# Attention of the first block: value matmuls with high and low halves side by side, and a shifted order of steps

## What is computed

```python
kc = rmsnorm(compress(heads(kcm, KVH), ...), ...)     # 31 compressed keys
vc = compress(heads(vcm, KVH), ...)                   # 31 compressed values
p_cmp = masked_softmax(einsum(q_nope, kc) * scale, cmp_mask)
o_cmp = einsum('bgntc,bgcd->bgntd', p_cmp, vc)
o_slc = selected_attn(q_rope, k_sl, heads(vsl, KVH), sel, scale)
o_win = window_attn(q_rope, k_wn, heads(vwn, KVH), scale)
o_nsa = gates[0] * o_cmp + gates[1] * o_slc + gates[2] * o_win
y_nsa = o_nsa * jax.nn.silu(nz)
```

## Time and profile before

| | us |
|---|---|
| median of 3 runs (lowest to highest) | 2809.46 (2808.98 to 2810.98) |
| profiled execution, its own time | 2808.89 |
| its span, first to last instruction | 2807.1 |
| PE busy | 2705.7 |
| DVE busy | 1167.6 |
| ACT busy | 1275.7 |
| POOL busy | 1402.6 |

### The profile page before, as it was taken

The page is one execution under the profiler, slowest core; times in us unless marked ns, Lnnn a source line. Parts: engine busy times, 40 slices in busy tenths (PEclk is TensorE's granted clock), DMA queues, the critical chain, the costliest instruction groups (busy, mean ns, idle before and its releaser), DMA issues.

```text
span 2807.1 us, 41389 instructions
## 1 busy us (share of the span) xinstructions
PE 2705.7 (96%) x13644; PEld 2276.7 (81%) x13644; DVE 1167.6 (42%) x2054; ACT 1275.7 (45%) x2207; POOL 1402.6 (50%) x1801
## 2 busy tenths in 40 slices
PE   8999899999889999999999999999999999999998
PEld 6888778788877888888878888888888887888887
DVE  4768742567874224423242422322442324142232
ACT  5555745655673643444443432324344444343233
POOL 4535554543554453554634655545355463455553
PEclk9999999999999999999999999999999999999999
DMA  5223013322301332233422333333223342233332
GB/s 153 72 50 99 16 39 90 91 61 65 92 1 54 89 110 69 90 98 98 124 87 69 106 104 91 98 98 110 69 90 98 98 124 88 68 106 105 91 98 98
DMA packets 270818, 242.46 MB, mean 86 GB/s; under 512 B 29376, under 2 KB 203648, under 8 KB 270592
## 3 DMA queue, kind: packets, MB, share of 16 engines
q1 hardware_dynamic: 267696, 235.12, 28.9%
q10 hardware_dynamic: 2896, 4.52, 0.5%
HBM read 237.51 MB, written 2.10 MB: 85 GB/s over the span
## 4 chain that ended last, share of the span: by engine, by line
PE 85%; DVE 6%; issue 4%; ACT 4%; DMA 0%; DVEq 0%; POOL 0%; ACTq 0%; POOLq 0%
PE bank L2017 11%; PE bank L2021 11%; PE bank L2020 11%; PE bank L1951 8%; PE bank L1954 8%; PE bank L1955 8%; PE bank L845 4%; PE bank L849 4%; PE bank L848 4%; PE bank L983 2%; PE bank L1906 2%; PE bank L895 1%; PE bank L898 1%; PE bank L899 1%; PE bank L2142 1%
## 5 line engine op out<-in xcount | busy, mean ns | idle before, releaser
L2865 POOL TENSOR_TENSOR wboth<-raw,wboth 128x256 fp32r<-128x256 f32 (+1 forms) x1616 | 1292.3, 832 | 1289.4 <-ACT wboth L2166 1289.1
L2166 ACT CAST wboth<-raw 128x1024 fp32r<-128x1024 f32 (+2 forms) x443 | 455.4, 1034 | 601.2 <-PE bank L2017 401.9
L1951 PE MATMUL bank<-xhi,wboth 128*128 128x512 f32 x928 | 364.2, 392 | 2.1 <-DVE h L2553 1.6
L1955 PE MATMUL bank<-xhi,wboth 128*128 128x512 f32 x928 | 361.4, 389 | 0.0
L1954 PE MATMUL bank<-xlo,wboth 128*128 128x512 f32 x928 | 361.3, 389 | 0.0
L2017 PE MATMUL bank<-wboth,xhi 128*128 128x512 f32 x832 | 326.5, 392 | 3.9 <-DVE xlo L2444 3.9
L2021 PE MATMUL bank<-wboth,xlo 128*128 128x512 f32 x832 | 324.0, 389 | 0.0
L2020 PE MATMUL bank<-wboth,xhi 128*128 128x512 f32 x832 | 323.8, 389 | 0.0
L845 PE MATMUL bank<-wboth,xhi 128*128 128x512 f32 (+2 forms) x672 | 248.2, 369 | 5.5 <-DVE pT L1524 3.1
L848 PE MATMUL bank<-wboth,xhi 128*128 128x512 f32 (+2 forms) x672 | 243.4, 362 | 0.0
L849 PE MATMUL bank<-wboth,xlo 128*128 128x512 f32 (+2 forms) x672 | 243.4, 362 | 0.0
(11 more groups left out here) (512 smaller groups left out, 4878.2 us busy)
## 6 DMA issues: line engine op xcount, KB each, us to landing
raw<-in_w_in SPq DMA_DIRECT2D x147, 512.0 KB, 3.7
raw<-in_w SPq DMA_DIRECT2D x132, 512.0 KB, 3.8
raw<-in_w_pg SPq DMA_DIRECT2D x16, 512.0 KB, 3.8
raw<-in_w_o SPq DMA_DIRECT2D x16, 512.0 KB, 3.8
raw<-in_xa_k SPq DMA_DIRECT2D x16, 512.0 KB, 3.9
raw<-in_xa_v SPq DMA_DIRECT2D x16, 512.0 KB, 3.9
raw<-in_xa_q SPq DMA_DIRECT2D x16, 512.0 KB, 4.1
raw<-in_xa_o SPq DMA_DIRECT2D x16, 512.0 KB, 3.8
```

The costliest lines, as they stand in the source:

```text
L1951: mm = pe.matmul(o, wh, rhs[0][:, k, :], start=(k == 0), stop=False)
L1955: mm = pe.matmul(o, wl, rhs[0][:, k, :], start=False, stop=(k == KD - 1))
L2166: nc.scalar.copy(whi[:, j % SLOTS, 0:nk * cols], raw[:, j % SLOTS, 0:nk * cols]).then_inc(hi_split, 1)
L2865: ins = nc.gpsimd.tensor_tensor(wlo[:, s, part], raw[:, s, part], whi[:, s, part].bitcast(F32), ALU.subtract)
```

## The change

- `value` takes two passes instead of three. A new tensor `vst` holds for each key tile, branch and group the 64 high columns beside the 64 low ones. The stationary operand is that pair, and it meets `Pt` high and `Pt` low. Rows 0 to 63 of the bank are then the sum with the high values and rows 64 to 127 that with the low values.
- `c_val` likewise takes two passes instead of four, with `vcp` laid out by group. The product low by low, left out before, is now included in both.
- `y_part` must add the two halves of the bank: ACT copies rows 64 to 127 into the other `y` buffer, DVE adds rows 0 to 63 to it, and then DVE multiplies by the gate, now from SBUF.
- In `attention_steps` a tile's compressed chain gets an empty slot after `c_weigh` and one after `c_split`. It begins in the tile before: at the first turn of unit (`g` 1, `br` 0) for `qt` 1, and at turn `kt` = 0 or 1 of unit (1, 1) for `qt` 2 and 3.
- Ahead of the attention `c_hid` and `c_back` of the second half come before `q_rope`, and both `nz_exp`/`nz_gate` 0 and 1 come after `c_out`.
- POOL writes `vst` in the same two instructions of 1024 elements a partition, with a strided output.

```diff
-        return [("c_score", qt), ("c_exp", qt), ("c_weigh", qt), ("c_split", qt), ("c_turn", qt)]
+        return [("c_score", qt), ("c_exp", qt), ("c_weigh", qt), None, ("c_split", qt), None, ("c_turn", qt)]
...
-            if qt and kt == 0 and (g, br) == (0, 0):
-                compressed = compressed_steps(qt)
+            if qt < TT - 1 and kt == qt // 2 and (g, br) == (1, qt > 0):
+                compressed = compressed_steps(qt + 1)
...
-    s += hid[0] + [("k_turn",), ("c_back", 0), ("q_rope",)] + hid[1] + [("nz_exp", 0), ("nz_gate", 0), ("c_back", 1)]
-    s += [("nz_exp", 1), ("c_out",), ("nz_gate", 1)]
+    s += hid[0] + [("k_turn",), ("c_back", 0)] + hid[1] + [("c_back", 1), ("q_rope",), ("c_out",)]
+    s += [("nz_exp", 0), ("nz_gate", 0), ("nz_exp", 1), ("nz_gate", 1)]
...
-                    for a in range(2):
-                        mm = pe.matmul(o, vcp[:, b, a, :], pcT[:, g, :], start=False, stop=(b == a == 1))
+                    mm = pe.matmul(o, vcp[:, b, g].rearrange("p a d -> p (a d)"), pcT[:, g, :], start=False, stop=(b == 1))
...
-                pe.matmul(G.ps(name)[:, :], vhi[:, kt, br, :], Pt[:, slot, 0, :], start=(kt == 0 and br == 0), stop=False)
-                pe.matmul(G.ps(name)[:, :], vlo[:, kt, br, :], Pt[:, slot, 0, :], start=False, stop=False)
-                pe.matmul(G.ps(name)[:, :], vhi[:, kt, br, :], Pt[:, slot, 1, :], start=False, stop=False).then_inc(*v_done.up())
+                both = vst[:, (2 * kt + br) * NKV + g].rearrange("p a d -> p (a d)")
+                pe.matmul(G.ps(name)[:, :], both, Pt[:, slot, 0, :], start=(kt == 0 and br == 0), stop=False)
+                pe.matmul(G.ps(name)[:, :], both, Pt[:, slot, 1, :], start=False, stop=False).then_inc(*v_done.up())
...
             def step_y_part(step):
                 qt, g = step[1:]
+                act.wait_ge(*G.filled(("o_a", qt, g), l))
+                nc.scalar.copy(y[(qt + 1) % 2][GROUP[g], :], G.ps(("o_a", qt, g))[GROUP[1], :]).then_inc(*sigs["hi"].up())
...
-                dve.wait_ge(*G.filled(name, l))
-                tt_(by_head(y[qt % 2][part, :]), by_head(G.ps(name)[part, :]), nzs[part, :, at], ALU.mult).then_inc(*G.empty(name))
+                dve.wait_ge(*hi_s.next(l))
+                link(tt_(y[qt % 2][part, :], G.ps(name)[GROUP[0], :], y[(qt + 1) % 2][part, :], ALU.add))
+                tt_(by_head(y[qt % 2][part, :]), by_head(y[qt % 2][part, :]), nzs[part, :, at], ALU.mult).then_inc(*G.empty(name))
```

More of the change, by code:

```diff
@@ L645, in build @@
         pT = sb("pT", [P, 2, 2, T], F32R, one)
-        vhi, vlo = (sb(n, [P, TT, 2, P], F32R, one) for n in ("vhi", "vlo"))
+        vst = sb("vst", [P, TT * 2 * NKV, 2, DH], F32R, one)
         def p_row(j):
```

15 lines of the change are left out of this document (7 added, 8 removed).

## The result

The changed kernel takes 2814.72 us (median of 12 runs), the kernel before 2811.13 beside it: 3.6 us or 0.13% more. The ratio over all runs is 1.002, 95% interval 1.0012 to 1.0028; that is the ratio of the means, and two runs of the changed kernel, at 2820.0 and 2826.6 us, lift it above that of the medians. So the kernel is slower, by less than the 5.6 us that the prediction took for the least that it could tell from no change. I had forecast 2799.3, faster by 0.4%, with a range of 2787 to 2812; the time lies outside it.

What follows compares the result with a forecast made beforehand. PE bounds the kernel, with DVE close behind in the middle. Middle 3.2, front 0.2 and tail 1.7 us give 5.1 a layer, 10.2 for two: 2799.3 us against the median of 2809.46, range 2787 to 2812.

Steps and rivals of the forecast that it cites:

- The front: Attention's start up to the first low part of `Pt`: ACT fills it; gain 0.2 us a layer.
- rival (d): Front: later `c_key` and gates delay ACT 1.5 us; 2806 to 2812; chance 0.17 together with rival (c).
- The waits of `c_turn`: Middle of the attention: PE's 6.9 us of waits for the low part of `c_split` go.
- DVE's work: Middle: six additions add 4.3 us, busy time 62.4 to 66.7 us; DVE becomes the bound instead of PE.
- collisions: Middle: DVE's gate products with two SBUF inputs lose time beside POOL; 0.35 us each, 2.1 us for six.
- DVE's wait for ACT's cast: Middle: of DVE's 11.4 us of waiting for ACT's cast of `Pt`, 3.0 us stay.
- w: Middle: what remains of DVE's 11.4 us wait for ACT's cast; a layer changes by -6.9 + w + unearned credit.
- rival (b): Middle: DVE's wait for ACT's cast stays as a latency; 2821 or 2816 us; chance 0.13.
- credit: End of the middle: turn 34 comes earlier against DVE's work because PE runs ahead; 1.2 us.
- rival (c): PE's clock falls more often while waiting for DVE; 2804 to 2811 us; chance 0.17 together with rival (d).
- The end: Tail from turn 34, PE alone at its limit: fewer value and `c_val` passes save 1.7 us a layer.
- my own case: Whole kernel: w from 1 to 5, front within 1 us of its value; 2791 to 2805 us, chance 0.60.

Runs made afterwards that it cites:

- e2_slots: Kernel before with only the compressed chain started earlier and two slots longer; 2804.7 us, ratio 0.9973 to 0.9991.
- e10_psum_sum: e4_no_front with the sum of the halves written back into the PSUM bank and the gate product reading it there; 2808.3 us, ratio 0.9983 to 1.0001.
- e4_no_front: Changed kernel with the old order ahead of the attention; 2810.7 us, ratio 0.9987 to 1.0005.
- e3_stack: Kernel before with only the stacked values (two passes, two for `c_val`, ACT copy, DVE addition, gate product); 2817.2 us, ratio 1.0009 to 1.0028.
- e6_nofront_bank: Changed kernel with the old order ahead of the attention and both groups of `c_turn` in one bank; 2797.5 us, ratio 0.9942 to 0.9969.
- g2_fill_turn: e3_stack with 16, 10, 10 and 40 identity transposes while PE waits in `c_turn`; 2808.8 us, ratio to the kernel before 0.9984 to 1.0002.
- g1_fill_score: Kernel before with only the new front order, plus 28 identity transposes while PE waits before `c_score` 0; 2819.9 us, ratio 1.0018 to 1.0041.
- f2_turn_only: Kernel before with only `q_rope` moved behind `c_back` 1; 2817.1 us, ratio 1.0018 to 1.0041.
- f3_gates_only: Kernel before with only `nz_exp` and `nz_gate` of tiles 0 and 1 moved behind `c_out`; 2814.1 us, ratio 1.0003 to 1.0021.
- g3_qt3_bank_fill: Longer slots, only the last tile stacked, `c_turn` in one bank (2785.7 us), plus 34 identity transposes before `c_back` 1; 2787.0 us.

## Why the prediction was wrong, point by point

**The front** (forecast -0.2 us a layer, bounds -2.0 to +1.5) measured +2.3 and +1.4. The term was mis-sized, and this is rival (d), to which I gave little. I had followed ACT's order and had `c_key` at 291.6; the copies came at 292.78 less the 1.8 us by which this run was late ahead of the change, so 291.0. I had the first `exp` 0.3 us later than before; it came 27.3 us after the start of the turns for 27.0. Both steps were right. What failed is the next one: from there on I kept the old durations, and the clock at nothing. PE's wait of 3.45 us was followed by about 10 us at half rate, and ACT waited for it the 1.82 and 1.78 us above. From `c_score` 0 to the first cast of `Pt` the changed kernel takes 13.9 us and e2_slots, with the old order, 11.2; so the order took back the 1.9 us that the `c_turn` 0 gave which left the front, and more. Taken alone the order costs 7.6 us in the whole kernel.

**The waits of `c_turn`** (forecast: gone, 6.9 us) came back as 7.3 us at turns and `c_turn` in e2_slots. The failed step is the sentence that these waits go, with its reason that PE is never more than two slots ahead of DVE because `value` waits for the low part. PE is held back earlier, by the three banks that turns share with the compressed chain; I did not read which steps share a bank. One edit to that is worth 11 to 13 us, more than all that I had forecast.

**DVE's work** was right in size: the six additions forecast at 4.3 us took 4.1, and the products grew by 0.6 where 2.1 stood for collisions. The 5.6 us measured (67.88 for 62.27) match the sum of 4.3 and up to 2.1 partly by luck: about 1.2 of them are a low part of `c_split` that the slots moved from the front into the middle, a shift that the forecast put at nothing. The 2.1 us of wait for the cast of `y` were kept, and PE was no longer the fullest engine. What failed is the step from there to the time, the middle's 72.7 us for 80.7 measured: I took DVE to be the bound with 3.9 us of idle left, and it had 12.8. A wait of DVE for ACT's new copy, costed at nothing, is 1.1 of them (1.2 in e10_psum_sum and e4_no_front, 2.4 in e3_stack).

**DVE's wait for ACT's cast** (forecast 3.0 us left of 11.4) is 7.6, past the point w = 5.7 from which rival (b) decides. That point is itself a slip: the -6.9 holds no credit, so a credit that isn't earned adds nothing to it. A layer changes by -6.9 + w, w decides from 6.9 us on, and the two times given for (b), 2821 and 2816, should be 2818 and 2814. The 7.6 is past either point. It gives 0.7 us a layer and 1.4 in all for the 3.6 measured, near by luck: against (b) the middle of layer 0 is 2.2 us and the front 2.5 us longer, and the end 2.8 us shorter. With the banks free it is 4.6 us in e6_nofront_bank. So part of it was neither a loop nor PE's work, but PE held back by a bank; the rival had the right side, and its reason, a latency of DVE and ACT, was incomplete.

**The clock** (rival (c), two or three spells of 1.3 us) is a cause of its own in the stacked middle: 3.0 us a layer by the profiles of g2_fill_turn, 8.4 us for the kernel by the medians. It is one in the reordered front too, by the profile of g1_fill_score. I had put the clock beside the sum as a chance, and not into it, though the sum itself made PE wait.

**The end** (forecast -1.7) is better than forecast: -0.9 by `p_turn`, then -3.6 and -2.8. A part is again the clock. The seven us from `p_turn` on, first before, then after:

```profile
393.00:400.00 7.00, 5.44 (x21) 4.36 (x22) 1.82 (x3) 2.12 (x3) 3.19 (x6) 0.76 0.25 75
```

```profile
401.00:408.00 7.00, 5.44 (x28) 4.43 (x29) 1.70 (x3) 2.13 (x3) 3.47 (x5) 1.00 0.25 77
```

The same busy time holds 28 matmuls instead of 21, 7 x 0.23 = 1.6 us won (28 for 22 in layer 1, 1.4 us), with the same wait of 1.56 us in it. e2_slots has 1.00 there too; why the spell misses these kernels isn't settled.

**The sum.** Slots -5.7, stack +6.8 and front +3.3 on top make 4.4 for the 3.6 us measured; since the front's 3.3 is itself taken from the changed kernel, only the 1.1 for 0.3 of the first two is a test. Of the prediction's own sums one end doesn't follow either: w of 1 and a front 1 us better give 2793, not the 2791 at which my own case begins. What the tests leave open: why the front costs 7.6 us alone and 3.3 with the rest (a later start may be absorbed by the waits that the stack has anyway; that was only argued); why f2_turn_only and f3_gates_only each have one middle, in layer 0, 4.5 and 6.0 us longer, at clocks of 0.94 and 0.92, while that of layer 1 is as before; how the stack's cost divides between DVE's addition and ACT's copy; and how much of the stack's 4.2 us with one bank is the clock, since no fill was tried there.

## What to carry to other kernels

These rules come from this one kernel. Before costing a wait at nothing, list which steps share the resource (here three PSUM banks) that is next in line, and ask who empties it: moving a step later in the chain only renames the wait if the same engine empties what it needs. Work taken from the fullest engine pays only in the stretch where that engine is alone at its limit; where a second engine is as near as here (62.4 us of work for 67.9), price each addition to it in full and apply the change to the other part alone. An engine that becomes the fullest by the sum is not thereby the bound: count the idle time that it has today, and name for each wait what takes it away. Where a sum makes PE wait, put the half-rate matmuls behind the wait into the sum as a term.

## What the runs showed of the hardware

**A wait costs PE more than its length.** A wait of 1.3 to 5.4 us was often followed by some 3 to 10 us at 1.2 GHz, so that an 80 us stretch had a granted clock of 0.86 to 0.92 for 0.98. Transposes of the identity put into the wait brought most of it back (0.86 to 0.96 and 0.91 to 0.98 in g2_fill_turn, 0.67 to 1.00 over 13 us in g1_fill_score). In the profiles that was worth 3.0 us a layer in the stacked middle and 2.5 to 3.0 us behind `c_score` 0; in the medians only g2_fill_turn gained, and g1_fill_score and g3_qt3_bank_fill stood 1.9 and 1.3 us higher, within the spread of their runs. The page TensorE: Matmul & The Clock Gate of the Trainium skill, section "A second HAM failure mode: psum-queue depth-cycling", describes a kernel in which frequent micro-idling of PE between groups of matmuls makes the clock swing between its levels. It gives no length of such an idle; that single waits of this length are followed by the lower level is what these traces add, and they agree with it.

**It is not certain each time.** The same wait of 3.6 us at the last `c_turn` was followed by full rate in the kernel before and by half rate in f2_turn_only. Six us behind it, first before, then f2_turn_only:

```profile
370.00:376.00 6.00, 6.00 (x36) 4.59 (x37) 3.86 (x9) 4.00 (x10) 2.24 (x4) 1.00 0.02 4
```

```profile
374.00:380.00 6.00, 6.00 (x27) 4.49 (x27) 2.66 (x6) 2.94 (x7) 1.23 (x2) 0.72 0.02 4
```

PE is busy the whole time in both, with 36 instructions or with 27. So an edit that only shifts the work in time can win or lose 9 matmuls here, in one profiled run of each.
